# Receptance, keys and values of an encoder layer by seven products of quarters in place of whole tiles

## The reference, cut to what matters

```python
hn = rms_norm(h, norm_mix)
proj = hn @ w_in                    # (256, 2048) @ (2048, ...)
u_r, q, k, v = _split(proj, (RWKV_COLS, ATT_WIDTH, ATT_KV_WIDTH, ATT_KV_WIDTH))
u_r = centred_shift(u_r, shift_prev, shift_next)     # u + mu_p*(u[t-1]-u) + mu_n*(u[t+1]-u)
y_r = rwkv7_bidirectional(u_r, ...)  # r, k, v are the first 3*1024 columns of u_r
y_a = rms_norm(window_attention(q, k, v, sink, bias), att_out_gain)   # 16 heads, 2 blocks of 128 queries
h = h + concatenate([y_r, y_a]) @ w_out
h = h + memory_cross_attention(rms_norm(h), rms_norm(mem), ...)
h = h + hierarchical_moe(rms_norm(h), ...)           # 32 experts, 3 matrices of 4 MB each
```

## Time and profile before

| | |
|---|---|
| median of three runs | 1781.48 us |
| profiled execution, its own time | 1781.07 us |
| its span on the core | 1778.9 us |
| PE busy in the span | 1693.4 us (95%) |
| DVE busy in the span | 642.8 us (36%) |
| the stage of the 24 tiles | 159 us to 363 us |
| DVE busy from 185 to 350 us | 61.0 us of 165 |
| POOL busy from 185 to 350 us | 5.8 us of 165 |

### The profile page before, as it was taken

The page is one execution under the profiler, slowest core; times in us unless marked ns, Lnnn a source line. Parts: engine busy times, 40 slices in busy tenths (PEclk is TensorE's granted clock), DMA queues, the critical chain, the costliest instruction groups (busy, mean ns, idle before and its releaser), DMA issues.

```text
span 1778.9 us, 36767 instructions
## 1 busy us (share of the span) xinstructions
PE 1693.4 (95%) x15777; PEld 1135.1 (64%) x15777; DVE 642.8 (36%) x1351; ACT 340.8 (19%) x977; POOL 117.5 (7%) x206
## 2 busy tenths in 40 slices
PE   9999999989989999999999999999999999999996
PEld 9887888877777788866555554445454545454543
DVE  2001333488885557323223323132223222322233
ACT  2122222157666101121000000000000000000002
POOL 1000000013233000001000000000000000000000
PEclk9999999999999999999999999999999999999999
DMA  9932434300000935546999999999999999999995
GB/s 314 213 114 95 121 116 171 120 3 4 4 4 4 352 139 179 213 189 239 413 395 426 432 427 431 429 432 430 430 429 432 428 430 430 430 431 426 404 422 224
DMA packets 101217, 503.61 MB, mean 283 GB/s; under 512 B 38253, under 2 KB 42881, under 8 KB 82161
## 3 DMA queue, kind: packets, MB, share of 16 engines
q1 hardware_dynamic: 96392, 489.78, 68.6%
q0 software_dynamic: 4464, 12.03, 2.4%
q10 hardware_dynamic: 248, 0.09, 0.0%
HBM read 511.29 MB, written 4.23 MB: 290 GB/s over the span
## 4 chain that ended last, share of the span: by engine, by line
PE 71%; DMA 21%; DVE 3%; issue 2%; SPq 1%; ACT 1%; POOL 1%; DVEq 0%; ACTq 0%; POOLq 0%; PEldq 0%
PE ps L1763 15%; DMA ring<-in_wu 10%; PE ps L2341 8%; PE ps L2093 8%; PE ps L2333 8%; PE ps L2484 8%; DMA ring<-in_wd 7%; PE ps L2349 4%; DMA rest<-in_wd 2%; PE ps L2220 2%; PE ps L2237 2%; DMA ring<-in_wg 1%; PE ps L1980 1%; PE ps L1975 1%; PE ps L2324 1%
## 5 line engine op out<-in xcount | busy, mean ns | idle before, releaser
L1763 PE MATMUL ps<-wide,ring 128*128 128x256 f32 x1248 | 275.3, 379 | 1.2 <-PE ps L1763 0.9
L1763 PEld LDWEIGHTS ps<-wide,ring 128*128 128x128 f32 x1248 | 239.0, 195 | 39.7 <-issue 10.1
L1621 DVE TENSOR_TENSOR tokA<-tokA,ps 128x512 f32<-128x512 f32 x256 | 158.4, 680 | 102.7 <-PE ps L2349 102.7
L2341 PE MATMUL ps<-ring,wide 128*64 128x256 f32 x1472 | 175.4, 399 | 20.3 <-DMA ring<-in_wu 20.3
L1634 DVE SCALAR_TENSOR_TENSOR gg<-ps,tmp,gg 128x256 f32<-128x256 f32 x32 | 15.5, 484 | 472.4 <-PE ps L2341 472.4
L2333 PE MATMUL ps<-ring,wide 128*64 128x256 f32 x1600 | 178.8, 381 | 2.8 <-DVE wide L1609 2.0
L2484 PE MATMUL ps<-ring,gg 128*64 128x512 f32 x736 | 168.1, 598 | 3.3 <-DMA ring<-in_wd 3.3
L2341 PEld LDWEIGHTS ps<-ring,wide 128*64 128x64 f32 x1472 | 110.8, 144 | 83.3 <-DMA ring<-in_wu 25.8
L2333 PEld LDWEIGHTS ps<-ring,wide 128*64 128x64 f32 x1600 | 113.6, 137 | 60.2 <-DVE wide L1609 3.4
L2349 PE MATMUL ps<-wide,gg 64*128 64x512 f32 x512 | 135.3, 627 | 0.6 <-ACT wide L944 0.6
L2484 PEld LDWEIGHTS ps<-ring,gg 128*64 128x64 f32 x736 | 48.7, 136 | 117.2 <-issue 106.1
(11 more groups left out here) (389 smaller groups left out, 2167.2 us busy)
## 6 DMA issues: line engine op xcount, KB each, us to landing
ring<-in_wu SPq DMA_DIRECT2D x20, 4096.0 KB, 28.5
ring<-in_wg SPq DMA_DIRECT2D x19, 4096.0 KB, 28.6
ring<-in_wd SPq DMA_DIRECT2D x19, 4096.0 KB, 30.5
rest<-in_wd SPq DMA_DIRECT2D x8, 4096.0 KB, 32.9
ring<-in_w_in SPq DMA_DIRECT2D x7, 4096.0 KB, 16.2
rest<-in_wg SPq DMA_DIRECT2D x6, 4096.0 KB, 27.0
rest<-in_wu SPq DMA_DIRECT2D x6, 4096.0 KB, 30.3
ring<-in_w_out SPq DMA_DIRECT2D x4, 4096.0 KB, 18.5
```

Of the source, the lines that this page charges most:

```text
L1621: V.tensor_tensor(fin_part(t, h, n), fin_part(t, h, n), ps[:, banks[q][h], :], ALU.add).then_inc(S["added"], 1)
L1763: ins = mm(ps[0:rows_, m % 2, 0:T], lhs, hnT[:, k, :], start=k == 0, stop=k == KD - 1)
L2341: ins = mm(ps[CAP * h:CAP * h + CAP, 1, 0:T], xT[:, k, CAP * i:CAP * i + CAP], w[:, T * h:T * h + T], start=k == 0, stop=k == KD - 1)
```

## The change

The six blocks of 512 columns are each computed as a product of two 2x2 matrices of quarters: tokens in two halves of 128, k in two halves of eight k-blocks, columns in two halves of 256. Seven products of eight matmuls take the place of eight such products. The stationary operand is now a 128x128 piece of rows (or of a sum of rows), the moving one 256 columns of weights (or of a sum of weights), so that the result stands with tokens on the partitions. It has to be turned: two transposes for each of the 24 tiles (`turn_tile`), in place, from and back to `rkv` by way of PSUM bank 7, ACT (`turned_raw`) and the unchanged `shift`.

The sums of weights are made in the slot itself. Three of each block are on DVE (`p_sum`), the fourth on POOL (`fourth_sum`), between its bias loads. Four sums of rows are made once (`row_sums`). DVE puts the seven products together in ten additions or copies (`p_op`). Blocks come in the order 0, 2, 4, 5, 3, 1. Scores, turned probabilities and values have one PSUM bank each in place of two. `keys(1)` and `quotients(1)` move from behind the stage into step 22. On SP, the load of the last six k-blocks of expert 1's up matrix, `put_ahead(4)`, 1.5 MB, moves from behind the wait for `gathered` to behind the wait for the stores of the rows (`h_out`).

```diff
+        BLOCK = (0, 2, 4, 5, 3, 1)
+        TILE = [4 * n + c for n in BLOCK for c in (2, 3, 0, 1)]
...
+            sp.wait_ge(S["h_out"], 16 + 16 * TB)
+            put_ahead(4)
             sp.wait_ge(S["gathered"], 16)
-            put_ahead(4)
             put_ahead(3)
...
+            def fourth_sum(i):
+                pool.wait_ge(S["p_sums"], 4 + P_SUMS * i + 3)
+                pool.tensor_tensor(W_B21(i - NB_), W_B21(i - NB_), W_B22(i - NB_), ALU.subtract).then_inc(S["p_t4"], 1)
+
             for jq in range(8):
                 if jq >= 2:
                     pool.wait_ge(S["sc_sum"], 2 * jq - 2)
...
+                if jq in (2, 4, 6):
+                    fourth_sum(jq // 2 - 1)
+            for i in range(3, NB_):
+                fourth_sum(i)
 
             pool.wait_ge(S["ya_done"], 18)
             pool.wait_ge(S["ya_sq"], 3)
+            pool.wait_ge(S["op_add"], P_ADDS * NB_)
             pool.memset(late[:, 3072:5632], 0.0).then_inc(S["zeroed"], 1)
...
+            def projection_block(i):
+                t0 = 4 * BLOCK[i]
...
+                p_op(X_U, made_product(1, 1))
+                p_sum(i, 1)
+                if i:
+                    projected(4 * i - 2)
+                    projected(4 * i - 1)
+                attention_step(4 * i)
+                p_op(rows_at(0, 0), X_U, made_product(2, 2))
+                p_sum(i, 2)
+                p_op(rows_at(0, 1), made_product(3, 3))
+                p_sum(i, 3)
+                attention_step(4 * i + 1)
+                five = made_product(4, 5)
+                p_op(rows_at(0, 1), rows_at(0, 1), five)
+                p_op(rows_at(1, 1), five)
+                attention_step(4 * i + 2)
+                p_op(X_U, X_U, made_product(6, 6))
+                p_op(rows_at(0, 1), rows_at(0, 1), X_U)
+                p_op(X_U, X_U, made_product(6, 7))
+                p_op(rows_at(1, 1), rows_at(1, 1), X_U)
+                p_op(rows_at(1, 0), X_U, made_product(7, 4))
+                attention_step(4 * i + 3)
+                projected(4 * i)
+                projected(4 * i + 1)
...
+            def turn_tile(s):
+
+                pe.wait_ge(S["op_add"], P_ADDS * (s // 4) + (9 if s % 4 < 2 else 10))
+                pe.wait_ge(S["tile_ev"], 17 + s // 2 * 2)
...
+            ORDER = (1, 2, 3, 5, 7, 6, 4)
+            for i in range(NB_):
+                landing(5 + i)
+                for step in range(7 * CT):
+                    q, k = ORDER[step // CT], step % CT
+                    if k == 0:
+                        ready(i, q)
+                    ins = mm(ps[:, P_BANK[q], 0:T], x_part(q, k), W_PART[q](i - NB_)[:, k], start=k == 0, stop=k == CT - 1)
+                    if k == CT - 1:
+                        ins.then_inc(S["op_mm"], 1)
+                    if step == CT - 1 and i:
+                        turn_tile(4 * i - 2)
+                        turn_tile(4 * i - 1)
...
+                    if step % 14 == 13:
+                        attention_step(4 * i + step // 14)
+                turn_tile(4 * i)
+                turn_tile(4 * i + 1)
```

More of the change, by code:

```diff
@@ L1079, in _, with projected @@
[L1079 to L1088, removed]
+            def projected(s):
+                shift(17 + s, 5 + s, rkv[:, TILE[s], :], TILE[s], P, sht if s < 16 else sht_late)
@@ L1296, in pair_ @@
                 V.tensor_tensor(Yp[:, 0:T - CH], Yp[:, 0:T - CH], ps[:, 7, T:2 * T - CH], ALU.add).then_inc(S["rw_yp"], 1)
[L1299 to L1330, removed]
-            projected(23)
+            def attention_step(j):
+                if 2 <= j <= 17:
+                    o_out(j - 2)
+                if j < 16:
+                    biased(j)
+                if j == 17:
+                    dve.wait_ge(S["sc_max"], 16)
+                    V.tensor_tensor(skt, negm, sinkb.unsqueeze(1).broadcast_to([P, 2, AH]), ALU.add).then_inc(S["sc_sum"], 1)
+                if j == 18:
+                    normalised()
+                    keys(0)
+                    for z in range(2):
+                        sums(0, z)
+                    middles()
+                    about()
+                    before(0)
+                if j == 19:
+                    dve.wait_ge(S["std_done"], 1)
+                    for b in range(TB):
+                        V.tensor_scalar(ya[:, b, :], ya[:, b, :], stat(4, 2)[:, b:b + 1], None, ALU.mult).then_inc(S["ya_hn"], 1)
+                if j == 20:
+                    dve.wait_ge(S["rw_n2"], 1)
+                    square_sums(ps[:, 6, 0:T])
+                    for part in range(2):
+                        scaled_keys(0, part)
+                    bonus_terms(0)
+                if j == 21:
+                    key_norms(0)
+                    unit_keys()
+                    for z in range(2):
+                        products_ar(0, z)
+                        products_bk(0, z, signal=False)
+                    dc.sync()
+                    V.tensor_copy(gam_now, gam).then_inc(S["rw_gnow"], 1)
+                    dve.wait_ge(S["rw_gnow"], 1)
+                    for z in range(2):
+                        products_out(z)
+                if j == 22:
+                    dve.wait_ge(S["rw_bon"], 1)
+                    bonus(0, ps[:, 6, 0:T])
+                    dc.sync()
+                    dve.sem_inc(S["rw_prep"], 1)
+                    keys(1)
+                    quotients(1)
@@ L1332, in _ @@
+            dve.wait_ge(S["rel_in"], 64)
+            row_sums()
+            for i in range(NB_):
+                projection_block(i)
+            projected(4 * NB_ - 2)
+            projected(4 * NB_ - 1)
             for n in range(4):
@@ L1848, in _, with attention_step @@
             ones2 = cst[:, BO:BO + P]
-            for j in range(24):
-                n = 5 + j // 4
-                if j % 4 == 0:
-                    landing(n)
-                tile(17 + j, cols(where[n], F, P * (j % 4), P))
-                if j % 4 == 3:
-                    leave(where[n], 18 + j)
-                if j == 0:
-                    pe.wait_ge(S["lora_ev"], CT)
+            def attention_step(j):
                 if 2 <= j <= 17:
```

175 lines of the change are left out of this document (133 added, 42 removed).

## The result

The changed kernel takes 1789.3 us (median of 12 runs, 1787.4 to 1791.1), the kernel before 1781.7 in the same comparison: ratio 1.0037, 95% interval 1.0029 to 1.0045. It is slower by 0.37%, within the 0.5% that the prediction counted as no change.

What follows compares the result with a forecast made beforehand. PE was taken to set the stage's time, with DVE turning critical at its end; -15.4 + 1.4 + 4.2 + 1.7 + 1.1 + 9.1 + 1.5 = +3.6 on 1781.07 gave 1784.7 us, range 1769 to 1796.

Steps and rivals of the forecast that it cites:

- PE's work: Whole stage on PE: 48 fewer matmuls, -20.7 us, and 48 added transposes, +5.3 us; together -15.4 us if nobody waits.
- block 3: GpSimd's sum starts right behind DVE's third; the small maximum of `biased(13)` waits 3.6 us, PE has 2.2 of room: +1.4 us.
- block 4: DVE, held by GpSimd's sum, finishes the ninth addition late for `turn_tile(16)`: +4.2 us, and half clock afterwards +1.7.
- block 5: PE waits 1.1 us for the fourth sum, then for DVE's last additions at 36.8 us: +1.1 and +9.1 us.
- tail: From turning the attention's rows to L1946: 11.2 us against 9.7 before, with DVE's shifts and POOL's memset ahead: +1.5 us.
- The close race: Blocks 0 to 2: the last small instruction of `biased` starts 0.06 us before GpSimd's sum can, so the hold costs nothing.
- rival 2: GpSimd's sum gets ahead of `biased`'s last instruction in blocks 0 to 2: +8.4 to +13.5, 1793 to 1798 us; chance 0.14.
- main case: GpSimd's sum holds DVE in blocks 3 to 5 only: 1784.7 us, own range 1779 to 1791; chance 0.50.
- no such wait in blocks 0 to 2: Sign in the changed trace: PE waits of about 4 and 9 us before L1980, but none in blocks 0 to 2.
- L1946's successor: Sign at the stage's end on PE: the instruction comes about 4 us later than 373.04.
- The hold itself: Each DVE instruction with two SBUF operands waits until GpSimd's fourth sum, taken as 5.1 us, is over; PSUM reads don't.
- Loads: The earlier `put_ahead(4)` load falls where DMA had room: 0 us, at most 4.7 us.

Runs made afterwards that it cites:

- the run with the later sum: Against the changed kernel, GpSimd's fourth sums of blocks 0 to 3 wait for the negation ending the step's bias chain: 1776.5 us, ratio 0.9970 to the kernel before.

## Why the prediction was right, and where it was not

The forecast was no change, 1784.7 us, and it is 1789.3: inside the range, 4.6 above the point. The terms, against the profiled execution before (us):

| term | predicted | measured |
|---|---|---|
| PE's work | -15.4 | -18.4 |
| blocks 0 to 2 | 0 | +6.5 waits, +5.2 half clock |
| block 3 | +1.4 | +0.2 |
| block 4 | +4.2, clock +1.7 | +2.0, clock +1.6 |
| block 5 | +1.1, +9.1 | 0, +8.8 |
| tail | +1.5 | +5.4 |
| the stage's first product 1.1 us earlier | | -1.1 |
| sum | +3.6 | +10.2 |

Half clock is what a block's stretch of PE is longer than in the run with the later sum, less the wait; work and tail are stretches of after less those of before; the tail begins behind the first pair of the last turned tiles.

**PE's work** was mis-sized by 3.0. 336 products at 0.432 are 145.2 us, and stand at 145.3; but the old tiles took 168.6 from start to start, not 165.8. At the end of each of the six blocks PE waited for its own last matmul before it handed the place on (the 0.30 us, released by PE, in the earlier trace rows), and that tile took 7.2 to 7.4 us in place of 6.91. In the changed kernel the turned tiles stand there, and the trace shows no such wait. I read one tile from inside a block and multiplied. (By the run without the sum, PE's work is another 0.4 us less.)

**The close race was lost**: this is the step that failed. "DVE is through by 0.06 us", I wrote, from the recorded starts. The maximum even started 0.28 to 0.37 us before the sum, and was held all the same. The mechanism and its place stood in rival 2, at a chance of 0.14; its waits, 2.8 us three times by the estimate, were 2.96, 1.75 and 1.77, and with the clock, which fell behind the first and the third, it cost 11.7 us, within the rival's 8.4 to 13.5. The result is the main case's blocks 3 to 5 with rival 2's blocks 0 to 2; it stays below the rival's 1793 because other terms came out lower. Of the signs that I had named, "no such wait in blocks 0 to 2" failed, and L1946's successor came 10.2 us later and not 4.

**The hold itself** was right in its length: the DVE instructions that it caught waited to the end of GpSimd's, and those that read PSUM weren't caught. The Trainium skill's rule (SBUF — State Buffer, "Who interferes with whom"), an exclusive lock on the shared ports, agrees with these rows in the whole instruction. Two operands in SBUF are not the whole condition: instructions with one tensor in SBUF were held too (L1071 by the memset; the negation for 2.28 us by the second half of the sum), and L1401 with two was not. The Trainium skill's "whoever issues first", said there of the 2-port modes, can't be applied to recorded starts: in block 5 step 21's first instruction (L1249, 350.27) starts 0.16 us before the sum and isn't held, in block 1 the maximum starts 0.28 before and is. What stands ahead of the sum differs: in blocks 0 to 2 it follows another GpSimd instruction at once, and there the maximum was held from up to 0.41 us ahead; in blocks 4 and 5 GpSimd had waited for DVE's third sum, and there L1249, and L1401 at 0.04 us behind the start, went free (in all seven traces with that sum on GpSimd). No run separates this from the kind of instruction. GpSimd's duration was 4.5 us, not 5.1; the Trainium skill's 4497 ns (GPSIMD Engine Reference, section 3.1) agree with the trace. The shorter sum took 0.5 to 0.6 from each hold.

**Block 3** cost 0.2 us. In blocks 1 and 2 a delay of 4.7 us (4.84 less the maximum's own 0.16) cost PE 1.75 and 1.77, so its room was 2.9 us, not 2.2, and block 3's delay is 2.9 (3.07 less 0.16), not 3.6. **Block 4** was mis-sized by 2.2: I let DVE wait for the whole sum and then do the sink terms (L1401) and two additions, 1.1 us, but these lie beside the sum, which itself was 0.5 us shorter; that is 1.6 of the 2.2, and the rest I can't assign. The clock's +1.7 was charged to a wait of 4.2 us and came with one of 2.0. **Block 5** was 8.8 for 10.2 in all; the fourth sum was ready in time.

**The tail** was mis-sized by 3.9. I charged the lower clock behind block 4's wait and left it out behind a wait of 8.8 us, though the earlier trace rows show it behind 2.76. From 367 to 373 us the clock is 0.53 and from 377 to 383 it is 0.51: 16 transposes take 3.4 us in place of 1.8. The memset held the first shift for 1.1 us (1.43 less its own 0.35), near the 1.2 of the prediction.

**Loads**: 0 us was right within what a run can tell.

So the errors of -3.0 (PE's work), +11.7 (blocks 0 to 2), -4.9 (blocks 3, 4 and 5), +3.9 (tail) and -1.1 (an earlier start) cancelled in part, and the point was better than its parts. That is luck: the lost race alone, put on the forecast, makes 1796.4 us, above the 1790.4 up to which I counted no change. Not settled is what decides the clock behind short waits: 1.99 us left it up in one kernel and not in another, and in the run with DVE's order in block 5 changed, two waits of 1.77 us went different ways (granted clock 1.00 from 221.4 to 225.4 us, 0.57 from 257 to 261).

## What to carry to other kernels

An elementwise instruction given to GpSimd isn't free for DVE: a DVE instruction on operands in SBUF that is caught by it waits for its end, so place it behind the short chain that others wait for (one semaphore wait was worth 13 us here), or keep it on DVE if DVE has the time to spare for its own instruction, here half as long (14 us). Margins of tenths of a microsecond between two engines, read from recorded starts, are no margins. Where DVE is full up to the point that counts, reordering mostly moves the largest wait of PE (from 8.83 to 0.91 us, for 2 us of time), and gave back no more than DVE's own gaps here; read the sum of DVE's work up to that point first, and look for work that another engine can take.

## What the runs showed of the hardware that I had not expected

A DVE instruction of 0.16 us took 4.8 to 5.0 us beside a GpSimd instruction that the trace shows starting 0.28 to 0.41 us later; at 0.49 us it wasn't held, nor were two others at 0.16 and 0.29 us, nor one that started 0.04 us behind it. Two GpSimd instructions back to back held it over both (4.98 us for 4.66), but not where it came while the first was running (0.90 us). Waits of PE of 1.75 to 2.96 us were followed by a lower granted clock in four of five cases of the kernel after; the same wait of 1.99 us was followed by full clock in the kernel with the later sum.
